# Summing the modulation vectors of a two-layer diffusion block: GpSimd's multiply and adds replaced by fused multiply-adds on VectorE

## The reference, cut to what matters

```python
silu_c = jax.nn.silu(c)                                   # (1, 1024)
for l in range(2):
    mod_lat = (silu_c @ ada_w[l] + ada_b[l])[:, None, :]  # ada_w[l] is (1024, 6144)
    sh1, sc1, g1, sh2, sc2, g2 = jnp.split(mod_lat, 6, axis=-1)
    a_lat = modulate(rms_norm(x, mix_norm[l]), sh1, sc1)
    # layer 0: attention and short convolution (even_mixer); layer 1: pooling mixer
    x = x + g1 * y_lat
    f_lat = modulate(rms_norm(x, ffn_norm[l]), sh2, sc2)
    x = x + g2 * conv_glu(f_lat, ffn_w_up[l], ffn_conv_w[l], ffn_conv_b[l], ffn_w_down[l])
```

## Time and profile before

| | us |
|---|---|
| median of 3 runs (1250.73 to 1255.97) | 1250.97 |
| span of the profiled execution | 1251.2 |
| TensorE busy | 1076.4 |
| VectorE busy | 748.0 |
| GpSimd busy | 485.2 |
| ScalarE busy | 416.9 |

### The profile page before, as it was taken

How to read it: one execution, slowest core, us unless ns; L and a number is a source line. 1 busy time by engine, 2 the same in 40 slices (tenths; PEclk the granted TensorE clock), 3 DMA queues, 4 the chain that set the end, 5 groups by cost and what they waited for, 6 DMA issues and landing times.

```text
span 1251.2 us, 13400 instructions
## 1 busy us (share of the span) xinstructions
PE 1076.4 (86%) x4684; PEld 852.4 (68%) x4684; DVE 748.0 (60%) x741; ACT 416.9 (33%) x534; POOL 485.2 (39%) x319
## 2 busy tenths in 40 slices
PE   5859779877976988999989987835999999999997
PEld 2349656665765766887767876723788888888876
DVE  1595776768586667536774476698544434443452
ACT  3432233333222543223231232333454223422332
POOL 0081563568465788608883289141100000000000
PEclk9888889999996999999999998966999999999999
DMA  8631232343344454525544344401232323342322
GB/s 289 229 101 64 85 101 92 94 133 89 110 139 118 119 149 154 182 68 164 154 151 143 110 129 131 127 1 34 67 101 100 102 80 89 100 126 76 92 76 68
DMA packets 152700, 141.87 MB, mean 113 GB/s; under 512 B 4738, under 2 KB 137432, under 8 KB 152664
## 3 DMA queue, kind: packets, MB, share of 16 engines
q1 hardware_dynamic: 140672, 99.27, 26.1%
q0 software_dynamic: 11520, 41.95, 11.2%
q10 hardware_dynamic: 472, 0.18, 0.1%
HBM read 139.28 MB, written 2.10 MB: 113 GB/s over the span
## 4 chain that ended last, share of the span: by engine, by line
PE 62%; DVE 22%; issue 5%; POOL 5%; ACT 4%; DMA 1%; ACTq 0%; DVEq 0%; POOLq 0%; SPq 0%
PE pair L526 18%; PE pair L527 18%; PE pair L528 18%; DVE w_lo L1089 5%; POOL acc L471 3%; DVE a_lo L1145 2%; POOL ada_raw L459 2%; DVE cb L1361 1%; PE pT L600 1%; DVE tmp L1135 1%; DVE tmp L1122 1%; DVE h_lo L1089 1%; PE pT L735 1%; DVE cb L1365 1%; DVE tmp L1288 1%
## 5 line engine op out<-in xcount | busy, mean ns | idle before, releaser
L526 PE MATMUL pair<-a_hi,w_hi 128*128 128x512 f32 x864 | 356.5, 413 | 80.8 <-DVE w_lo L1089 24.8
L527 PE MATMUL pair<-a_lo,w_hi 128*128 128x512 f32 x864 | 349.6, 405 | 0.0
L528 PE MATMUL pair<-a_hi,w_lo 128*128 128x512 f32 x864 | 348.5, 403 | 0.0
L1089 DVE TENSOR_TENSOR w_lo<-w_raw,w_hi 128x2048 fp32r<-128x2048 f32 (+1 forms) x119 | 232.1, 1957 | 48.1 <-ACT w_hi L813 35.2
L526 PEld LDWEIGHTS pair<-a_hi,w_hi 128*128 128x128 f32 x864 | 170.2, 197 | 128.3 <-issue 39.1
L471 POOL TENSOR_TENSOR acc<-acc,ada_raw 128x512 f32<-128x512 f32 x120 | 204.2, 1702 | 9.4
L528 PEld LDWEIGHTS pair<-a_hi,w_lo 128*128 128x128 f32 x864 | 170.0, 197 | 37.6
L527 PEld LDWEIGHTS pair<-a_lo,w_hi 128*128 128x128 f32 x864 | 170.5, 197 | 34.6 <-issue 0.5
L526 PE MATMUL pair<-h_hi,w_hi 128*128 128x512 f32 (+1 forms) x432 | 170.0, 394 | 14.1 <-DVE w_lo L1089 11.1
L813 ACT ACTIVATE w_hi<-w_raw 128x2048 fp32r<-128x2048 f32 x68 | 129.6, 1906 | 128.3 <-PE pair L528 128.3
L527 PE MATMUL pair<-h_lo,w_hi 128*128 128x512 f32 (+1 forms) x432 | 167.7, 388 | 0.0
(11 more groups left out here) (212 smaller groups left out, 1017.8 us busy)
## 6 DMA issues: line engine op xcount, KB each, us to landing
w_raw<-in_ffn_w_up_dram SPq DMA_DIRECT2D x88, 512.0 KB, 5.0
ada_raw<-in_ada_w_dram POOLq DMA_DIRECT2D x80, 512.0 KB, 4.1
w_raw<-in_ffn_w_down_dram SPq DMA_DIRECT2D x32, 512.0 KB, 4.4
w_raw<-in_even_w_in_dram SPq DMA_DIRECT2D x20, 512.0 KB, 4.6
w_raw<-in_ffn_w_down_dram SPq DMA_DIRECT2D x16, 384.0 KB, 3.9
w_raw<-in_ada_w_dram SPq DMA_DIRECT2D x10, 512.0 KB, 4.9
w_raw<-in_even_w_out_dram SPq DMA_DIRECT2D x8, 512.0 KB, 4.6
ada_raw<-in_ada_w_dram SPq DMA_DIRECT2D x6, 512.0 KB, 6.4
```

The lines of the kernel that those rows point to most:

```text
L526: nc.tensor.matmul(dst, lh, rh, start=start, stop=False)
L527: nc.tensor.matmul(dst, lh, rl, start=False, stop=False)
L528: return nc.tensor.matmul(dst, ll, rh, start=False, stop=stop)
L1089: return nc.vector.tensor_tensor(dst, full, hi.bitcast(f32), ALU.subtract)
```

## The change

GpSimd keeps the chunk loads alone: for each it waits until VectorE has used the chunk whose buffer it takes (`ada_fma`). VectorE does each chunk with two instructions of 128x512: a `scalar_tensor_tensor` that multiplies a half by its `silu_c` value and adds it to `acc`, and for the first half of a block a `tensor_scalar` multiply. `acc` alternates between two buffers in the mixer. In the mixer the 36 chunks of blocks 0 to 8 stand every 2.8 steps, from step 5 to step 103 of 112, and a block's transposes stand three steps behind its last chunk. In the first feed-forward part every up slot takes two chunks, one ahead of the split of the next weights (`lo_next`) and one behind it, for the block after the one that is reduced in the same trip; the transposes move from step 4 to step 1 of the trip's second slot. So block 8, the first of layer 1, is now summed within the mixer.

```diff
-    ada_steps = {(2, 0): 0, (3, 4): 1, (5, 4): 2, (7, 0): 3, (8, 4): 4, (9, 4): 5, (11, 4): 6, (13, 6): 7}
+    chunk_steps = {}
+    for ch in range(4 * (ADA0 + 1)):
+        chunk_steps[5 + 14 * ch // 5] = ch
+    ada_steps = {8 + 14 * (4 * b + 3) // 5: b for b in range(ADA0)}
...
-            if (n, k) in ada_steps:
-                s.append(("ada", ada_steps[n, k]))
+            if 8 * n + k in chunk_steps:
+                s.append(("fma", chunk_steps[8 * n + k]))
+            if 8 * n + k in ada_steps:
+                s.append(("ada", ada_steps[8 * n + k]))
...
-            def ada_sum(b, src, col_block, next_src, next_block, first=False):
+            def chunks_after(b, src, col_block, next_src, next_block):
 
                 for q in range(4):
-                    w = ada_raw[:, q % 2, :].rearrange("p (k n) -> p k n", k=2)
-                    pool.wait_ge(ada_loaded[q % 2], 32 * b + 16 * (q // 2 + 1))
-                    nc.gpsimd.tensor_tensor(w, w, silu_c[:, 2 * q:2 * q + 2].unsqueeze(2).to_broadcast([P, 2, SEQ]),
-                                            ALU.mult).then_inc(prod_done, 1)
...
                     if q < 2 or next_src is not None:
-                        pool.wait_ge(acc_done, 7 * b + 2 * q + 1)
+                        pool.wait_ge(ada_fma, 8 * b + 2 * q + 2)
...
-            def ada_reduce(b, use):
-
-                pe.wait_ge(acc_done, 7 * b + 7)
+            def ada_reduce(b, v, use):
+
+                pe.wait_ge(ada_fma, 8 * b + 8)
...
-                                if l == 0 and u == 1 and k == 4:
-                                    ada_reduce(ADA0 + j0 // 2 + i, T_FFN0 + j0 // 2 + i)
+                                if l == 0 and u == 1 and k == 1:
+                                    ada_reduce(ADA0 + j0 // 2 + i, 0, T_FFN0 + j0 // 2 + i)
...
+            def ada_chunk(b, v, q, free=None):
+
+                dve.wait_ge(ada_loaded[q % 2], 32 * b + 16 * (q // 2 + 1))
+                for kk in range(2):
+                    k = 2 * q + kk
+                    w = ada_raw[:, q % 2, kk * SEQ:(kk + 1) * SEQ]
+                    if k == 0:
+                        if free is not None:
+                            dve.wait_ge(ada_ready, free)
+                        nc.vector.tensor_scalar(acc[:, v, :], w, silu_c[:, 0:1], None, ALU.mult).then_inc(ada_fma, 1)
+                    else:
+                        dve.wait_ge(ada_fma, 8 * b + k)
+                        nc.vector.scalar_tensor_tensor(out=acc[:, v, :], in0=w, scalar=silu_c[:, k:k + 1],
+                                                       in1=acc[:, v, :], op0=ALU.mult, op1=ALU.add)\
+                            .then_inc(ada_fma, 1)
...
+                if kind == "fma":
+                    b = unit[1] // 4
+                    ada_chunk(b, b % 2, unit[1] % 4, b - 1 if b >= 2 else None)
+                elif kind == "ada":
...
                             lo(h_lo[:, 2 * i + u, :], cb[:, v, :], h_hi[:, 2 * i + u, :]).then_inc(h_ready, 1)
+                            if l == 0:
+                                ada_chunk(ADA0 + 1 + j0 // 2 + i, 0, 2 * u, ADA0 + 1 + j0 // 2 + i)
                             lo_next(s)
+                            if l == 0:
+                                ada_chunk(ADA0 + 1 + j0 // 2 + i, 0, 2 * u + 1)
```

More of the change, by code:

```diff
@@ L111, in mixer_schedule @@
     return s
+ADA0 = 8
+ADA1 = 12
 MIX = mixer_schedule()
@@ L241, in build @@
         aux_read = [sem(f"aux_read{i}") for i in range(3)]
-        prod_done = sem("prod_done")
-        acc_done = sem("acc_done")
+        ada_fma = sem("ada_fma")
         ada_ready = sem("ada_ready")
@@ L489, in _ @@
             lo_by_pool(1)
[L490 to L493, removed]
+            with pool.Fori(0, ADA0 - 1) as i:
+                chunks_after(i, src0, i + 4, src0, i + 5)
+            chunks_after(ADA0 - 1, src0, ADA0 + 3, src1, 0)
             with pool.Fori(0, ADA1 - 1) as i:
-                ada_sum(i + ADA0, src1, i, src1, i + 1)
-            ada_sum(ADA0 + ADA1 - 1, src1, ADA1 - 1, None, None)
+                chunks_after(i + ADA0, src1, i, src1, i + 1)
+            chunks_after(ADA0 + ADA1 - 1, src1, ADA1 - 1, None, None)
             pool.wait_ge(ada_ready, ADA0 + ADA1)
@@ L679, in ada_reduce @@
                 for i in range(4):
-                    ins = nc.tensor.transpose(pT[:, i * P:(i + 1) * P], acc[:, 0, i * P:(i + 1) * P], ident[:])
+                    ins = nc.tensor.transpose(pT[:, i * P:(i + 1) * P], acc[:, v, i * P:(i + 1) * P], ident[:])
                 ins.then_inc(ada_ready, 1)
@@ L687, in _ @@
                 elif kind == "ada":
-                    ada_reduce(unit[1], T_USE[unit])
+                    ada_reduce(unit[1], unit[1] % 2, T_USE[unit])
                 elif kind == "st":
@@ L778, in down @@
                                 if l == 0 and part == 2 and k == 4 and 2 * i + u == 3:
-                                    ada_reduce(ADA0 + ADA1 - 1, T_OUT - 1)
+                                    ada_reduce(ADA0 + ADA1 - 1, 0, T_OUT - 1)
                                 if last and k == 3 and 2 * i + u > 0:
@@ L1245, in _ @@
                 kind = unit[0]
-                if kind == "ada":
+                if kind == "fma":
+                    b = unit[1] // 4
+                    ada_chunk(b, b % 2, unit[1] % 4, b - 1 if b >= 2 else None)
+                elif kind == "ada":
                     at = 16 + 4 * unit[1]
```

2 lines of the change are left out of this document (removed).

## The result

The changed kernel takes 1159.22 us (median of 4 runs, 1158.35 to 1161.43) against 1250.98 us (4 runs). The ratio is 0.926, 95% interval 0.924 to 0.929: 92 us faster. The forecast was 1186 us with a range of 1163 to 1211; the sign and the mechanism were right, the size was short by 27 us, and the measured time lies 4 us beyond the range's fast end.

The account below looks back on a forecast made before the run. TensorE's matmuls were taken as the floor, busy 1076.4 of 1251.2 us, with its waits the question. Terms 11 + 5 + 0 + 6 + 2 + 41 + 1 - 1 = 65 gave 1186 us, range 1163 to 1211.

Parts of the forecast that it names:

- the start: From 76 us on, removing GpSimd's instructions shortens VectorE's L1211 work that TensorE waits for: 11 us gain, bounds 7 and 16.
- 92 to 146: Mixer from 92 to 146 us: less blocking of VectorE against its share of chunks, 5 us gain (0 to 8).
- first chunks: Mixer's first chunks: VectorE waits for loads to land, 1 us lost.
- 146 to 344: Mixer from 146 to 344 us: VectorE's load stays as it is, gain 0, bounds -23 and +12.
- mixer's end and the norm: 344 to 385.6 us: half of VectorE's 13 us of blocking is on the path, 6 us gain (3 to 10).
- first feed-forward slot: Layer 0's first feed-forward slot goes from 19.2 to layer 1's 17.1 us, 2 us gain.
- 29 slots: Layer 0's feed-forward slots from the second on: 364.4 us becomes 324, a gain of 41, bounds 28 and 47.
- last four slots: Last four slots of layer 0's feed-forward part: 1 us gain.
- late slots: Layer 0's feed-forward up trips: chunks on VectorE make some slots late, costing 1.5 us together.
- the mixer's gain: Rival: blocks on the path go, chunks fall into idle time, clock stays up; 12 us here, 5 at start; 1169 us, chance 0.15.
- The issues: Rival: GpSimd's load issues block VectorE's instructions with two SBUF operands, 12 us on the path; 1198 us, chance 0.09.
- Late chunks: Rival: chunks land late and VectorE stands at them, slower than before; 1265 us at 1 us each, chance 0.03.

Follow-up runs that it names:

- Run 2: The kernel before with GpSimd's 80 products and 120 adds cut to 8 columns, its order, waits and loads kept: 1138.42 us.
- runs 9 and 10: Changed kernel plus GpSimd passes over an idle tile ahead of 40 chunk issues, first feed-forward part: 1189.94 us (9); with a second pass each time, 1218.49 us (10).

## Why the prediction was right or wrong

The forecast's own terms against the lengths in the table (the same matmuls before and after). "Less idle" and "less busy" part the measured gain by TensorE's own rows; the busy time is that of the same matmuls, so its fall is mostly the clock:

| term | forecast gain | measured | less idle | less busy |
|---|---|---|---|---|
| mixer slots 0 to 2 ("the start", 92 to 146, first chunks) | 11 + 5 - 1 | 20.3 | 15.5 | 4.8 |
| mixer slots 3 to 11 (146 to 344) | 0 | 9.9 | 6.7 | 3.2 |
| mixer's end and the norm | 6 | 9.7 | 7.4 | 2.3 |
| first feed-forward slot | 2 | 5.0 | 2.2 | 2.8 |
| 29 slots | 41 | 43.4 | 28.6 | 14.8 |
| last four slots | 1 | 1.5 | | |
| pooling mixer and layer 1 | 0 | 0.8 | | |

**The mechanism** was right: one engine waits for the whole of the other's instruction. Run 2 removes most of it with the order of before kept, and runs 9 and 10 bring it back in the feed-forward part with the order and the waits of the changed kernel kept. For the mixer run 2 is the only such run.

**The feed-forward term** was right to 2.4 us, because it came from a stretch of the same work without GpSimd. The 1.5 us for late slots were too careful: TensorE shows no wait in the 29 slots, and all that they take beyond layer 1's 317.3 is 3.7 us, against 6.5 forecast for the transposes and the late slots together. The `tensor_scalar` of 512 elements takes 481 ns, against the 0.49 us estimated.

**The step that failed** is "From 146 to 344 I take 0". It read "VectorE's load stays as it is" as "the time stays". It is the largest of the misses: 9.9 of the 26 us that the terms together fell short. The load did stay: 138.8 us before, 133.9 after. But blocking cost 29.7 us there and the chunks 19.9, which is 0.8 us for each microsecond of VectorE's that blocking took and 0.6 for each that the chunks take. What is shown is the two prices; why a microsecond of blocking costs more is only argued: blocks stretch instructions that TensorE waits for, and bring two or three microseconds at once, while many chunks fall where VectorE was idle. The rival for this case, the mixer's gain, was right in sign and near in size (12 forecast, 9.9 measured), but had a chance of 0.15.

**The start and the norm** were short by 5.3 and 3.7 us. For the start that is the clock: the 15.5 us of idle time that went are the forecast's 15, and the 4.8 us of busy time are what it had kept only as a bound (5 us, from 11 to 16). The mean clock would say more than is there. In slots 0 to 2 it goes from 0.84 to 0.95, that is from 28.6 us at 1.2 GHz to 6.8, and half of the difference would be 11 us. But before, TensorE was busy for only half of those 28.6 us. These are their three pieces in the kernel before (length, PE, PEld, DVE, ACT, POOL, granted clock, DMA share, GB/s):

```profile
59.50:64.60 5.10, 5.10 (x12) 4.05 (x13) 4.83 (x7) 3.74 (x4) 0.34 (x1) 0.50 0.87 309
85.10:102.20 17.10, 9.79 (x34) 8.53 (x35) 12.35 (x16) 5.67 (x13) 8.36 (x6) 0.50 0.22 61
139.70:146.10 6.40, 0.03 (x1) 0.06 (x1) 6.40 (x7) 1.69 (x2) 3.81 (x3) 0.50 0.33 88
```

The low clock costs only while TensorE has work. At the mixer's end idle time fell by 7.4 us, more than the 6 of the forecast, and the clock gave 2.3. In the first feed-forward slot the forecast took the length of layer 1's, whose clock is 0.80, and got 0.86.

**The issues** block nothing, and here the reading of the earlier trace rows was wrong. The changed kernel has GpSimd issues with no GpSimd instruction behind them. In its timeline 48 instructions of VectorE begin inside an issue, and none takes over 0.01 us longer than the shortest of the same line and size. VectorE, then GpSimd:

```profile
372.37 0.16 DVE L1157 TENSOR_TENSOR mod<-modc,col 128x4 f32 x1 [0.28 <-DVE modc L1154]
372.54 0.75 DVE L1367 SCALAR_TENSOR_TENSOR cb<-gp,col,cb 128x512 f32<-128x512 f32 x1
```

```profile
372.14 0.72 POOL L455 DMA_DIRECT2D ada_raw<-in_ada_w_dram  x1 [2.92 <-DVE acc L1171]
```

L1367, with two large SBUF operands, starts 0.40 us into an issue and takes its 0.75 us. That agrees with what the Trainium skill states (SBUF — State Buffer, "Who interferes with whom"): VectorE with two SBUF inputs contends with a GpSimd instruction that reads SBUF, not with one that only writes it. In the earlier trace rows it was the multiply behind the issue that blocked; why it came first, though it began 0.30 us later, no run here settles.

**Late chunks**: the landing times stay at 4.2 us median and 7.1 at most, and VectorE waits 5.8 us in four pieces for loads in all. The Trainium skill's warning of starved descriptors (SBUF — State Buffer, "SBUF: two separate sides") is not tested here: in the changed kernel's timeline none of the 80 issues (724 ns median, 848 at most) runs beside one of VectorE's 20 `tensor_scalar` of 481 ns. The rival's time of 1265 us is a slip of the sum; 1186 and 80 times 1 us are 1266.

**The range** was too narrow at its fast end. It took the mixer's gain and stopped 6 us behind it, though the terms can gain together. Every term for which the prediction gave bounds was measured within them (7 to 16 with 0 to 8, -23 to +12, 3 to 10, 28 to 47), and their fast ends together give about 1156 us, beyond the measured span of 1159.8. So the step that made the range fail is the mixer's 0 together with a range that left no room for several terms to gain at once.

## What to carry to other kernels

Price work that moves between GpSimd and VectorE by two subtractions, the blocking that goes and the time that comes, each with short instructions in place of long ones; equal loads are not equal times. GpSimd's busy time alone doesn't give its harm: 118 us of it, placed behind each chunk, cost 31 us, and 213 us (244 with the issues) at the places of before cost 43. Compare busy times only as the trace has both, with the waiting in them. Moved pieces belong where TensorE is the bound (free in 29 slots here) and away from steps that share a PSUM bank. To price the clock, look at TensorE's busy time for the same matmuls and not at the mean clock.

## What was not expected of the hardware

- Much of the low clock is free: in the mixer's first slots before, 28.6 us were granted 1.2 GHz, but TensorE was busy in only 14.9 of them, and the clock's share of the 20.3 us gained there is at most the 4.8 us by which its busy time fell.
- Blocking shows on either side: in run 9 GpSimd's 1.9 us pass shows 3.86 us when `w_lo` is there first, and VectorE's pair of 1.53 us shows 3.17 when GpSimd is.
- In the changed kernel one instruction before the pooling mixer is still blocked: the `a_lo` at 63.84, which takes 4.61 us beside GpSimd's split of slot 1.

```profile
63.84 4.61 DVE L1132 SCALAR_TENSOR_TENSOR a_lo<-tmp,mod,a_hi 128x512 fp32r<-128x512 f32 x1 [0.32 <-ACT a_hi L832]
```
